# Tables' second rows 24 beats behind the first, in a one-core trunk step with nine ring places

## What is computed

```
q = (xb @ w_q)...; s = q . sub_keys             # 8 heads, two sets of 128 keys
top 16 of each set -> 256 sums -> best 16        # "routing": 8 x 16 = 128 experts a row
act = gelu(einsum('td,thkd->thk', xb, u_tab[idx]))
out = einsum('thk,thkd->td', g * act, v_tab[idx])
```

## Time and profile before

| | us |
|---|---|
| median of 3 runs | 4093.12 |
| lowest and highest | 4084.87 and 4098.61 |
| profiled execution, its own time | 4105.51 |
| span of its trace | 4103.7 |

### The profile page before, as it was taken

The page is one execution under the profiler, slowest core; times in us unless marked ns, Lnnn a source line. Parts: engine busy times, 40 slices in busy tenths (PEclk is TensorE's granted clock), DMA queues, the critical chain, the costliest instruction groups (busy, mean ns, idle before and its releaser), DMA issues.

```text
span 4103.7 us, 28498 instructions
## 1 busy us (share of the span) xinstructions
PE 3034.7 (74%) x7904; PEld 1357.0 (33%) x7904; DVE 2650.3 (65%) x5344; ACT 870.8 (21%) x1778; POOL 2373.0 (58%) x2218
## 2 busy tenths in 40 slices
PE   6899988987756776777677767776877687764566
PEld 4644433433223322332243234322432233321221
DVE  4214658675777576767676778676867665676544
ACT  4321211220122112211231123112311132111011
POOL 0100334465667566766676677656756676577776
PEclk9999999998988997889898988998989898997899
DMA  6543898899989998999899999998999999999998
GB/s 220 185 158 123 278 334 284 287 338 409 367 339 367 409 366 328 362 404 379 330 351 408 387 346 357 408 376 328 340 399 376 354 360 328 408 336 370 375 363 314
DMA packets 410545, 1390.19 MB, mean 339 GB/s; under 512 B 48493, under 2 KB 51565, under 8 KB 409197
## 3 DMA queue, kind: packets, MB, share of 16 engines
q0 software_dynamic: 316384, 1151.48, 74.5%
q1 hardware_dynamic: 74772, 200.96, 13.3%
q10 hardware_dynamic: 19232, 35.92, 2.4%
HBM read 1358.52 MB, written 29.66 MB: 338 GB/s over the span
## 4 chain that ended last, share of the span: by engine, by line
PE 25%; DMA 19%; POOL 16%; issue 14%; DVE 14%; another core or an unknown queue 4%; ACT 3%; SPq 0%; DVEq 0%; ACTq 0%; POOLq 0%
POOL t_ring L1162 16%; DMA t_ring<-in_peer_v,t_idx 11%; PE ps L1375 10%; PE ps L1388 5%; DVE t_ring L1899 5%; PE ps L1238 4%; DMA t_ring<-in_peer_u,t_idx 4%; DMA val<-in_w_in 2%; PE ps L1190 2%; DVE t_acc L1917 2%; PE ps L1215 1%; DMA t_big<-in_peer_w_query 1%; DMA t_big<-in_w_out 1%; DMA keyT<-in_cache_k_sb 1%
## 5 line engine op out<-in xcount | busy, mean ns | idle before, releaser
L1388 PE MATMUL ps<-t_ring,t_diag 128*128 128x512 f32 (+1 forms) x2696 | 1457.1, 672 | 613.9 <-DMA t_ring<-in_peer_v,t_idx 509.6
L1162 POOL DMA_INDIRECT t_ring<-in_peer_u,t_idx x1088 | 1153.9, 1061 | 1055.4 <-PE ps L1388 282.4
L1162 POOL DMA_INDIRECT t_ring<-in_peer_v,t_idx x1088 | 1199.5, 1102 | 497.7 <-issue 284.9
L1899 DVE CUSTOM_DVE_ANT_0 t_ring<-t_ring,ps 128x1024 f32<-128x1024 f32 x960 | 1158.2, 1214 | 379.4 <-DMA t_ring<-in_peer_u,t_idx 333.1
L1388 PEld LDWEIGHTS ps<-t_ring,t_diag 128*128 128x128 f32 (+1 forms) x2696 | 509.6, 207 | 1460.8 <-DMA t_ring<-in_peer_v,t_idx 886.6
L1917 DVE SCALAR_TENSOR_TENSOR t_acc<-t_ring,t_wgt,t_acc 128x1024 f32<-128x1024 f32 x413 | 531.1, 1286 | 194.5 <-DMA t_ring<-in_peer_v,t_idx 163.5
L1238 PE MATMUL ps<-t_big,t_pTr 128*128 128x512 f32 x864 | 428.1, 641 | 92.5 <-DMA t_big<-in_w_out 24.6
L1564 ACT ACTIVATE t_diag<-ident,t_wgt 128x128 f32<-128x128 f32 x645 | 248.9, 400 | 893.2 <-PE ps L1388 489.3
L1375 PE MATMUL ps<-val,keyT 128*128 128x512 f32 x800 | 368.8, 604 | 29.6 <-DMA val<-in_w_in 28.5
L1416 ACT COPY t_pTr<-ps 128x512 f32<-128x512 f32 (+3 forms) x216 | 111.1, 514 | 800.9 <-PE ps L1190 525.2
L1238 PEld LDWEIGHTS ps<-t_big,t_pTr 128*128 128x128 f32 x864 | 166.6, 203 | 338.1 <-issue 187.1
(11 more groups left out here) (215 smaller groups left out, 2177.8 us busy)
## 6 DMA issues: line engine op xcount, KB each, us to landing
t_big<-in_w_out SPq DMA_DIRECT2D x72, 512.0 KB
t_big<-in_peer_w_query SPq DMA_DIRECT2D x72, 512.0 KB
wraw<-in_w_in SPq DMA_DIRECT2D x40, 512.0 KB, 5.9
t_big<-in_w_proj_diff SPq DMA_DIRECT2D x36, 512.0 KB
val<-in_w_in ACTq DMA_DIRECT2D x36, 512.0 KB
t_big<-in_w_proj_sb SPq DMA_DIRECT2D x36, 512.0 KB
t_ring<-in_peer_u,t_idx POOLq DMA_INDIRECT x1088
t_ring<-in_peer_v,t_idx POOLq DMA_INDIRECT x1088
```

Of the source, the lines that this page charges most:

```text
L1162: pool.indirect_dma_start(row(kind, e, s), None, table, bass.IndirectOffsetOnAxis(ap=idx[:, e % 3, s:s + 1], axis=0)).then_inc(s_ring[g % ...
L1388: m = nc.tensor.matmul(ps[0:n, c, :], diag[:, v_place[e, s] % NDG, 0:n], row("v", e, s)[:, c * CH:(c + 1) * CH], start=v_first(e, s), stop ...
L1899: nc.vector.tensor_tensor_reduce(out=row("u", e, s), in0=row("u", e, s), in1=x_row, scale=1.0, scalar=0.0, op0=ALU.mult, op1=ALU.add, accu ...
```

## The change

- `VLAG` becomes 24 and is counted from u: slot s of tile e has its u at beat 6+s and its v at beat 30+s of the same turn e+1. All v work comes 112 beats earlier, and the schedule ends 112 beats earlier (1246 beats instead of 1358).
- Weights are made in groups of 16 slots (`GROUP`): `act_gelu` and `dve_weights` run 2 and 3 beats after the last dot of a group, 68 times in all instead of 9.
- The quarters move: 64 instead of 81 in turn 0, 112 instead of 116 in turn 1, 104 instead of 83 in turn 2, where they run at about one a beat up to beat 116. The last four chunks are split into tile 2 alone and then tiles 3 to 8, so weights are loaded for 14 groups instead of 10. Beside the routing of turns 1 and 2 the quarters use banks 2 and 3.
- `v_on_dve`: 470 v adds on DVE instead of 414. In turn 1 and up to beat 84 of turn 2 all v adds are on DVE, but for two of three in beats 85 to 123 of turn 1; in beats 85 to 127 of turn 2 one of three is on DVE. Tile 0's sum is joined at beat 2 of turn 2. From turn 3 on the pattern by beats is nearly as before. Join and finish move to beats 30 and 34 of turn e+2.
- `acc` holds two tiles; its third place becomes `wkept`, in which the first of the 24 merge blocks stays, loaded once instead of nine times. The ring keeps nine places.

```diff
-VLAG = 14
+VLAG = 24
+GROUP = 16
+JOIN_0 = 2
-        B_CHUNKS = (1, 2, 0, 4, 5, 3, 6, 7, 8, 9)
-        B_UNITS = [(c, t) for c in B_CHUNKS for t in B_TILES]
+        B_GROUPS = [(c, B_TILES) for c in (1, 2, 0, 4, 5, 3)]
+        B_GROUPS += [(c, B_TILES[:1]) for c in (6, 7, 8, 9)] + [(c, B_TILES[1:]) for c in (6, 7, 8, 9)]
+        B_UNITS = [(c, t) for c, tiles in B_GROUPS for t in tiles]
-            acc = sb("t_acc", [P, 3, D])
+            acc = sb("t_acc", [P, 2, D])
+            wkept = sb("t_wkept", [P, D])
...
             def u_at(beat):
-                return row_at(beat, 1, ULAG)
+                return row_at(beat, ULAG)
             def v_at(beat):
-                return row_at(beat, 2, VLAG)
+                return row_at(beat, ULAG + VLAG)
-            LAST_BEAT = (NPT + 2) * BEATS + VLAG + slots_of(NPT)
+            LAST_BEAT = (NPT + 1) * BEATS + ULAG + VLAG + slots_of(NPT)
...
+            quarter_beats = [b for b in range(2, MERGE_AT, 2)] + [b for b in range(MERGE_AT, KEYS_AT, 3)] + [b for b in range(KEYS_AT, KEYS_AT + 26)]
+            quarter_beats += [BEATS + b for b in range(MERGE_AT)] + [BEATS + b for b in range(MERGE_AT + 1, MERGE_AT + 20, 2)]
+            quarter_beats += [BEATS + b for b in range(KEYS_AT, KEYS_AT + 40)]
+            quarter_beats += sorted([2 * BEATS + b for b in range(JOIN_0 + 1, MERGE_AT)] + [2 * BEATS + b for b in (20, 30, 40)])
+            quarter_beats += [2 * BEATS + b for b in range(MERGE_AT + 1, MERGE_AT + 20, 2)] + [2 * BEATS + b for b in range(KEYS_AT, KEYS_AT + 32)]
...
             def v_on_dve(e, s):
                 n = slots_of(e)
-                turn, b = divmod((e + 2) * BEATS + VLAG + s, BEATS)
-                if (turn, b) < (FIRST, B_END):
-                    return True
+                turn, b = divmod((e + 1) * BEATS + ULAG + VLAG + s, BEATS)
+                if turn == 1 or e == 0 or (turn == 2 and b < KEYS_AT):
+                    return not (turn == 1 and KEYS_AT <= b < BEATS - 4) or s % 3 == 0
...
-                return b < MERGE_AT and s % 3 == 0
+                return (b < MERGE_AT or turn == 2) and s % 3 == 0
...
+            def act_gelu(act, e, g):
+                cols = slice(g * GROUP, (g + 1) * GROUP)
+                act.wait_ge(s_dot, e * NSLOT + (g + 1) * GROUP)
+                if e:
+                    act.wait_ge(s_wgt, weighed(e - 1, g))
+                nc.scalar.activation(act_u[:, cols], dots[:, e % 2, cols], ACT.Gelu).then_inc(s_gelu, 1)
```

More of the change, by code:

```diff
@@ L798, in slots_of, with row_at @@
                 return NSLOT // 2 if e == NPT else NSLOT
-            def row_at(beat, turns, lag):
-                e, s = divmod(beat - lag, BEATS)
-                return (e - turns, s) if 0 <= e - turns <= NPT and s < slots_of(e - turns) else None
+            def row_at(beat, lag):
+                e, s = divmod(beat - BEATS - lag, BEATS)
+                return (e, s) if 0 <= e <= NPT and s < slots_of(e) else None
             def u_at(beat):
-                return row_at(beat, 1, ULAG)
+                return row_at(beat, ULAG)
@@ L807, in v_at, with group_at, weighed @@
             def v_at(beat):
-                return row_at(beat, 2, VLAG)
-            LAST_BEAT = (NPT + 2) * BEATS + VLAG + slots_of(NPT)
+                return row_at(beat, ULAG + VLAG)
+            def group_at(beat, lag):
+                row = row_at(beat, ULAG + GROUP - 1 + lag)
+                return (row[0], row[1] // GROUP) if row and row[1] % GROUP == 0 else None
+            def weighed(e, g):
+                return e * (NSLOT // GROUP) + g + 1
+            LAST_BEAT = (NPT + 1) * BEATS + ULAG + VLAG + slots_of(NPT)
@@ new lines, in build, with beside_routing @@
+            quarter_beats += [2 * BEATS + b for b in range(MERGE_AT + 1, MERGE_AT + 20, 2)] + [2 * BEATS + b for b in range(KEYS_AT, KEYS_AT + 32)]
+            assert len(quarter_beats) == NQ
+            quarters = {}
+            for n, b in enumerate(quarter_beats):
+                quarters.setdefault(b, []).append(n)
+            def beside_routing(unit):
+                turn, b = divmod(quarter_beats[4 * unit], BEATS)
+                ends = divmod(quarter_beats[4 * unit + 3], BEATS)
+                assert not turn or (turn, b >= KEYS_AT) == (ends[0], ends[1] >= KEYS_AT)
+                return turn > 0 and b >= KEYS_AT
@@ L1556, in act_diag @@
                 k = v_place[e, s]
-                if v_first(e, s):
-                    act.wait_ge(s_wgt, e + 1)
-                    if is_sample(e):
-                        act.wait_ge(s_fold, 1)
+                if s == min(r for r in range(s // GROUP * GROUP, slots_of(e)) if not v_on_dve(e, r)):
+                    act.wait_ge(s_wgt, weighed(e, s // GROUP))
+                if v_first(e, s) and is_sample(e):
+                    act.wait_ge(s_fold, 1)
                 if k >= NDG:
@@ L1569, in act_program @@
                     turn, b = divmod(beat, BEATS)
-                    if b == ULAG and 1 <= turn <= NPT + 2:
+                    if b == ULAG and 1 <= turn <= NPT + 1 and turn != NPT:
                         e = turn - 1
-                        if e <= NPT and e != NPT - 1:
-                            if e:
-                                act.wait_ge(*dots_done(e - 1))
-                            act.wait_ge(s_xn, e + 1)
-                            nc.scalar.copy(both(4)[:, :], xn_of(e)).then_inc(s_xps, 1)
                         if e:
-                            cols = slice(0, slots_of(e - 1))
                             act.wait_ge(*dots_done(e - 1))
-                            nc.scalar.activation(act_u[:, cols], dots[:, (e - 1) % 2, cols], ACT.Gelu).then_inc(s_gelu, 1)
+                        act.wait_ge(s_xn, e + 1)
+                        nc.scalar.copy(both(4)[:, :], xn_of(e)).then_inc(s_xps, 1)
+                    if group_at(beat, 2):
+                        act_gelu(act, *group_at(beat, 2))
                     ahead = v_at(beat + DIAG_AHEAD)
@@ L1589, in act_program @@
                         act_piece(act, t, *piece)
-                    for n in quarters.get(beat, ()):
+                    for n in quarters.get(beat - 2, ()):
+                        act_store(act, n)
+                    for n in quarters.get(beat - 1, ()):
                         act_quarter(act, n)
```

158 lines of the change are left out of this document (93 added, 65 removed).

## The result

| | before | after |
|---|---|---|
| median, runs of the first comparison, us | 4089.0 | 3960.2 |
| profiled execution, span, us | 4103.7 | 3969.3 |

A second comparison, five rounds on another chip, gave 0.969 (0.967 to 0.972).

The account below looks back on a forecast made before the run. DMA time was taken as the bound, with slack mainly in turns 1 and 2. End -165, turn 0 -27, turn 1 +134, turn 2 +28, turns 3 to 8 -8: -38 on 4105.5, so 4067 us; range 4010 to 4115.

Parts of the forecast that it names:

- a turn is DMA time: Steady turns: DMA engines busy 0.99, 0.98, 1.03 and 0.90 of four stretches, slack only beside the routing; 1.39 us a gather.
- a ceiling read from turn 2: DMA share reachable with both streams: 0.94 in beats 23 to 61, 1.03 in the merge, 0.91 in the routing.
- +70: Turn 1, routing to beat 5: 189.7 us of DMA work, divided by 0.91, makes 208 us, 70 more.
- The first stretch: Turn 1, beats 30 to 61: 32 added gathers bring DMA work to 102.2 us, /0.94 = 109, so +45.
- The waits for weights of one-tile groups: Turn 2, tile 2's last four chunks: next load must land in three beats; taken as 0, bounds 0 to 20 us.
- The end: From beat 6 of turn 9: 112 fewer gathers at 1.473 us of elapsed time each, -165 us.
- Turn 0: Its last 17 quarters go, so PE no longer holds tile 1 and the gates end last: -27 us.
- Rival 1: Turns 1 and 2 don't pack, DMA shares stay: +215 for +162, total 4108 us; chance 0.2.
- Rival 3: Relief of DVE at the turns' start counts in full, 6.4 us in 6 turns: -38, 4017 us; chance 0.12.
- the three signs of being wrong: Share under 0.85 in turn 1's beats 85 to 133; turns 3 to 7 moving over 3 us each; DVE waiting for Gelus.
- Rival 2: Gelus hold DVE in turns 2 to 8: 21 x 2.57 us = 54, total 4109 us; chance 0.08.
- rival 4: Turn 0 gives nothing: 4082 us; chance 0.1.

Follow-up runs that it names:

- the two shorter ends named with the table: Two kernels that do there what the kernel before does: 382.2 and 379.9 us from beat 6 of turn 9 to the end.
- the groups of eight: The changed kernel with weights made in groups of 8 slots instead of 16, 136 Gelus instead of 68: 3970.0 us, ratio 0.970.
- the two runs that agree: The changed kernel with gathers of half a row, 3842.9 us, and without every fourth v gather of tiles 2 to 6, 3809.7 us.

## Why the prediction was wrong

**The step that failed is the first: "a turn is DMA time", with DMA busy time as the sum's currency.** The sum for turns 1 and 2 added 1.39 us of DMA busy time a gather to length times share and divided by a ceiling read from turn 2. 57 of the 99 us by which turns 1 and 2 were put too high lie in turn 1, in its merge and routing. In the merge the ceiling of 1.03 was met, but with 84.2 x 1.03 = 86.7 us of busy time instead of 97.1. In its routing stretch the busy time was 162.2 x 1.01 = 163.8 us instead of 189.7, and the ceiling 1.01 instead of 0.91. What was added comes out at about 0.9 us of busy time a gather in both. Before the change that stretch had a share of 0.83 at 292 GB/s; against the 408 GB/s of the merges that is a rate of 0.72, much more room than the share shows.

"A turn is DMA time" was read off the DMA share, 0.99, 0.98, 1.03 and 0.90 in a steady turn. A share near one doesn't say that no more would fit. The rate says more: 408 GB/s in the merges, 375 and 339 in the other stretches of the same turn, and 33 GB/s more went into the routing for nothing.

What paced these stretches stands in rows that the prediction didn't read. POOL in beats 23 to 61 of turn 3, kernel before: its groups, then what it waited for (us, times, longest).

```profile
L1162 POOL DMA_INDIRECT t_ring<-in_peer_u,t_idx x40 | 42.3, 1058 | 25.8 <-issue 15.2 <-PE ps L1388 6.8 <-remote 3.8
L1162 POOL DMA_INDIRECT t_ring<-in_peer_v,t_idx x40 | 38.9, 973 | 12.5 <-issue 11.3 <-DVE t_dots L1899 1.2
```

```profile
POOL t_ring L1162 <- issue: 26.5, 72, 4.3
POOL t_ring L1162 <- PE ps L1388: 6.8, 3, 3.3
```

81.2 us busy with issuing and 26.5 us of "issue" between two, 108 of 118 us; only 8 us went to waits for ring places and 4 to a release that the view doesn't name. A gather took 1.0 us to issue and 0.3 to go on to the next. POOL's 58% of the span leaves those gaps out, so the nearest limit wasn't seen. With half the bytes the record keeps its length; the changed kernel in beats 23 to 61 of turn 3, then the same with half rows:

```profile
L1201 POOL DMA_INDIRECT t_ring<-in_peer_u,t_idx x39 | 46.4, 1189 | 19.6 <-issue 10.7 <-PE ps L1446 8.9
```

```profile
L1201 POOL DMA_INDIRECT t_ring<-in_peer_u,t_idx x39 | 45.5, 1167 | 17.3 <-issue 11.3 <-PE ps L1450 3.3 <-remote 2.7
```

1.17 us for 1.19. The Trainium skill (Perfetto Trace Analysis, "DMA Instruction — SWDGE (GPSIMD)") says that such a record ends when the last descriptor is generated, not when the data has moved. The trace agrees: the record of a gather of 2 KB rows is as long as that of one of 4 KB rows.

**Turn 1.** Before the change POOL had time to spare there, because with u alone it waited for dots. Beats 85 to 5, kernel before, then changed kernel:

```profile
POOL t_ring L1162 <- DVE t_dots L1899: 70.9, 44, 19.4
POOL t_ring L1162 <- issue: 4.9, 7, 3.1
```

```profile
POOL t_ring L1201 <- issue: 30.6, 75, 3.9
POOL t_ring L1201 <- PE ps L1446: 11.6, 8, 3.1
POOL t_ring L1201 <- DVE t_dots L1965: 8.2, 11, 1.5
POOL t_ring L1201 <- DVE t_acc L1986: 5.6, 5, 1.2
```

71 of 138 us of waiting for dots became 25 us of waits for ring places (the last three rows) and 26 us more between two issues; 48 more gathers went through in 24 us more. The sum charged them 68 us of DMA time and divided by 0.91: +70, the largest error. The DMA engines reached 1.01 of share and 396 GB/s, so the ceiling of 0.91 belonged to the stretch that it was read from and not to the DMA engines; what sets the pace of that stretch is open. The merge (+9 for a forecast of +19) has the same fault. The first stretch came out right (+44 for +45). POOL didn't hold it: 64 gathers at 1.35 us are 86 of its 108 us. With half rows beats 23 to 61 of turn 1 fell from 121.5 to 101.0 us, so there bytes do count, and the sum's way gave the right number. A gather added 1.5 us of busy time there (121.5 x 0.98 less 78.1 x 0.90, over 32) and about 0.9 behind; why isn't shown.

**Turn 2.** The prediction saw that PE was full at two quarters a beat and gave back nothing for it: 0.94 was taken as the DMA engines' ceiling for beats 23 to 61, though the changed kernel reached 1.02 there and the kernel before with slower quarters 0.99. The latter with slower quarters shows 16 us in beats 6 to 61 without any lag. The waits for weights of one-tile groups, which the prediction put at 0 with a bound of 20, rose by 13 us (28.5 to 41.7), inside that bound. For the routing, the 14 adds on DVE were priced at 18 us; they cost nothing, as did 19 more a turn elsewhere.

**What was right, and why.** The end: -162 for -165 (-153 and -155 against the two shorter ends named with the table). It was priced by elapsed time per gather, 1.473 us, a measured pace that holds whatever its cause; the half rows show that the cause named was wrong. Turn 0: -25.5 for -27, through PE and the gates as described. Turns 3 to 8: -10 for -8, which says only that little changed; that it meets the 8 is luck, given 22 us between two readings of the same work. Covered Gelus: right. The kept block: at most 1 us a turn.

**The rivals.** Rival 1 had the sign of the error wrong: turns 1 and 2 packed better than forecast, not worse. Rival 3 looked for the upside at the turns' start; turns 3 to 8 show none. None of the three signs of being wrong caught the error: the share in beats 85 to 133 of turn 1 was 1.01, turns 3 to 7 moved by -3.5 to +2.9 us, and in the changed kernel's trace nothing waited for a Gelu. No sign was set for a share above the ceiling. No rival said "the bound is another engine's issue", although 71 us of POOL waiting in one stretch of turn 1 stood in the trace. At the merges' 408 GB/s the bytes of turns 1 and 2 as they came out (400.9 us at 388 GB/s, 426.0 at 392) need 381 and 409 us. Both turns ended 4 and 5% above that cap; the forecast of 458 us for turn 1 lay 20% above it. That was worked out only afterwards. Rival 2 fell with the groups of eight, rival 4 with the first dot at 401.5.

**Open.** Why a routing stretch gets longer with half rows (158.9 to 169.5) isn't settled, nor what its own floor is: it lost 12 us for 12 gathers fewer and nothing was added by 8 more loads or 14 more adds. That POOL's issuing sets beats 23 to 61 rests on the two runs that agree and on POOL's sum, not on a kernel in which issuing alone was made cheaper. That sum leaves about 10 of 117 us, and the chain followed back through these beats of turn 3, kernel before, runs through POOL's gathers for 26%, through pauses between instructions for 12% and through landings of gathers for 34%; so their landing time has a part too, although a tenth ring place gained nothing.

## What to carry to other kernels

A DMA busy share near one doesn't show a full DMA system: compare the rate of the stretch with the highest rate seen anywhere in the same trace, and add the issuing engine's gaps to its busy time before calling it idle. Don't add busy time of DMA engines as if each transfer had a fixed amount. To find what paces a stretch, halve the bytes and, apart from that, drop some of the instructions; where bytes bind, both shorten it, and where issuing binds, only the second does. Work moved out of a stretch gives back that stretch's elapsed time per piece, and costs in the new place only what the limit there, often another engine, charges.

## What the runs showed of the hardware

- Two rates for nearly the same share: 1.02 to 1.03 and 403 to 409 GB/s in the merges shown of turns with both streams, 0.97 to 0.98 and 362 to 375 GB/s in beats 23 to 61 of the steady turns shown.
- An indirect gather of 128 rows saved 1.0 to 1.2 us of time where it was left out, for rows of 4 KB; with rows of 2 KB beats 23 to 61 were 3 us of 120 shorter (7 of 118 in the kernel before). POOL needs 1.35 us for one by its records and pauses, and its 0.524 MB need 1.28 us at 408 GB/s, which is why the two limits were easy to take for each other.
- The same 316384 packets of queue 0 took 36 us less busy time in sum (3057 and 3021 us) in the shorter of two schedules. The reason wasn't looked for.
- Table loads of ACT are 1.283 us each; 39 more of them moved the time by at most 10 us.
